# Merge of layer 0 in chunks of 2, 4 and 4 tiles, with merge's first loads beside attention C and the modulation pieces later

## The reference

```
ya = gqa_attend(aq, k_a, v_a)                      # A: 8 heads
yb = diff_attend(bq, k_b, v_b, lam, subln)         # B: 4 heads, RMSNorm over 128 of the output
yc = windowed_latent(cq, ck, cv, xck, xcv, sink)   # C: 8 heads
g  = sigmoid(h @ w_in[gates]); ga, gb, gc = split(g, 3)
m  = ga * (ya @ w_branch_a) + gb * (yb @ w_branch_b) + gc * (yc @ w_branch_c)
x  = x + mod[2] * (m @ w_out)
mod = silu(c) @ w_ada + b_ada                      # one row of 6 * 1024 per layer and token kind
```

## Time and profile before

| what | us |
|---|---|
| median of 3 executions | 5331.33 |
| lowest and highest | 5330.62, 5336.91 |
| the profiled execution, its own time | 5333.29 |
| span of its profile | 5331.7 |
| TensorE busy | 4735.2 (89%) |
| VectorE busy | 3234.0 (61%) |
| ScalarE busy | 2625.5 (49%) |
| POOL busy | 1144.7 (21%) |
| mean granted TensorE clock | 0.948 of full |

### The profile page before, as it was taken

One profiled execution on the slowest core, in us unless ns is written; L12 is line 12 of the kernel. 1 busy time (PEld: TensorE's weight loads), 2 busy tenths in 40 slices (PEclk: granted clock), 3 DMA queues, 4 the chain that ended last, 5 costly groups with the idle time before them and its releaser, 6 DMA issues. The chain is left out here.

```text
span 5331.7 us, 85889 instructions
## 1 busy us (share of the span) xinstructions
PE 4735.2 (89%) x30278; PEld 4027.9 (76%) x30278; DVE 3234.0 (61%) x5512; ACT 2625.5 (49%) x3457; POOL 1144.7 (21%) x1082
## 2 busy tenths in 40 slices
PE   5889899889899977999984888999989998799996
PEld 2788787778678866887774888888868777587774
DVE  4554366767443456877767551667764435777776
ACT  2443355556332322777763442556652321577774
POOL 0542001440000002333333440015100001333333
PEclk7999999999899998999996999999989998899998
DMA  7432533544433455999996433433243327799998
GB/s 276 167 97 79 154 78 81 175 163 108 181 136 126 150 211 190 390 397 397 397 361 236 161 95 99 117 82 77 66 153 132 140 94 241 279 397 397 397 397 336
DMA packets 595821, 1094.75 MB, mean 205 GB/s; under 512 B 112177, under 2 KB 295729, under 8 KB 590497
## 3 DMA queue, kind: packets, MB, share of 16 engines
q1 hardware_dynamic: 551296, 940.52, 51.3%
q0 software_dynamic: 30816, 103.16, 5.1%
q10 hardware_dynamic: 13504, 48.39, 2.3%
HBM read 908.01 MB, written 183.95 MB: 205 GB/s over the span
## 5 line engine op out<-in xcount | busy, mean ns | idle before, releaser
L667 PE MATMUL project_proj_acc<-project_w_split,project_hT 128*128 128x256 f32 x5472 | 730.5, 294 | 3.2 <-DVE project_hT L526 2.9
L667 PEld LDWEIGHTS project_proj_acc<-project_w_split,project_hT 128*128 128x128 f32 x5472 | 699.2, 200 | 7.0 <-DVE project_hT L526 6.6
L1685 PE MATMUL merge_acc<-merge_hT,merge_w_split 128*128 128x512 f32 (+1 forms) x2880 | 641.3, 377 | 37.4 <-DMA merge_hT<-hT 31.0
L1685 PEld LDWEIGHTS merge_acc<-merge_hT,merge_w_split 128*128 128x128 f32 x2880 | 506.5, 191 | 147.6 <-issue 30.5
L2391 DVE TENSOR_TENSOR experts_w_gate<-experts_raw_gate,experts_w_gate 128x2048 fp32r<-128x2048 f32 x148 | 372.2, 2522 | 295.1 <-ACT experts_w_gate L2281 295.1
L2266 POOL TENSOR_TENSOR experts_w_down<-experts_raw_down,experts_w_down 128x2048 fp32r<-128x2048 f32 x74 | 357.2, 4826 | 534.7 <-ACT experts_w_down L2281 534.7
L2440 PE MATMUL experts_gate_acc<-experts_w_gate,experts_rowsT 128*128 128x512 f32 x1776 | 438.1, 402 | 12.8 <-DVE experts_rowsT L2396 7.1
L2454 PE MATMUL experts_result_acc<-experts_w_down,experts_hiddenT 128*128 128x512 f32 x1776 | 436.1, 401 | 12.2 <-DVE experts_w_down L2391 12.2
L971 DVE TENSOR_REDUCE attend_stat<-attend_scores 128x1 f32<-128x1280 f32 (+2 forms) x288 | 305.8, 1062 | 219.2 <-PE attend_scores L872 215.6
L2440 PE MATMUL experts_up_acc<-experts_w_up,experts_rowsT 128*128 128x512 f32 x1776 | 426.5, 395 | 0.0
L2440 PEld LDWEIGHTS experts_gate_acc<-experts_w_gate,experts_rowsT 128*128 128x128 f32 x1776 | 330.9, 190 | 102.7 <-issue 19.8
(11 more groups left out here) (236 smaller groups left out, 8163.8 us busy)
## 6 DMA issues: line engine op xcount, KB each, us to landing
experts_raw_gate<-in_w_exp_gate_dram SPq DMA_DIRECT2D x148, 1024.0 KB, 14.0
experts_raw_up<-in_w_exp_up_dram SPq DMA_DIRECT2D x148, 1024.0 KB, 12.8
experts_raw_down<-in_w_exp_down_dram SPq DMA_DIRECT2D x148, 1024.0 KB, 11.5
merge_w_raw<-in_w_merge_dram SPq DMA_DIRECT2D x120, 768.0 KB, 6.3
qk<-project_staged SPq DMA_DIRECT2D x168, 256.0 KB, 2.3
attend_keys<-qk SPq DMA_DIRECT2D x128, 320.0 KB, 6.0
ye<-experts_result ACTq DMA_DIRECT2D x74, 512.0 KB, 6.3
modulation_w_ada<-in_w_ada_dram SPq DMA_DIRECT2D x24, 1024.0 KB, 26.5
```

What stands on the lines that cost most here:

```text
L667: m = pe.matmul(acc[s % 2][:, 0:HALF], hT[:, a, k, t * P:(t + 1) * P], w_split[hf][:, c, k, :], start=(i == 0 and k == 0), stop=(i == 2 an ...
L1685: m = pe.matmul(acc[:, b, 0:w], w_split[b][:, a, k, :], hT[:, x, k, 0:w], start=(i == 0 and k == 0), stop=(i == 2 and k == KD - 1))
```

## The change

Two buffers now live through attend and merge of a layer. `wide` holds B's keys, then merge's hT; `rows` holds B's probabilities `p0` and `p1`, then merge's three `w_raw`. SP issues hT of tiles 0 to 3 (both halves, 2048 KB each) and the weights of the first three units once B's last step is done, ahead of C's stores and loads; merge itself loads only ident, y and gain before its loop. In both layers the queries and values of A's first head are issued by ScalarE, and SP issues only its keys. In layer 0 POOL waits for step 2 * nq of A's scores before the first two pieces of w_ada. Merge of layer 0 takes its tiles in chunks of 2, 4 and 4; in layer 1 the chunks stay 4 and 4. Since a chunk of two uses only y buffers 0 and 1, the count that a reader of a y buffer waits for is now worked out by `y_load`. The initial y loads stay four.

```diff
+MERGE_ROWS = (KD + 4) * P
@@ attend_gqa, loads
-        def load(i, b):
+        def load_keys(i, b):
...
+        def load_rest(i, b):
             sp.dma_start(queries[b][:, :].bitcast(F32),
...
+        def load(i, b):
+            load_keys(i, b)
+            load_rest(i, b)
@@ sync_first
+            load(0, 0)
+        else:
+            load_keys(0, 0)
         load(0, 1)
+    def scalar_first(act):
+        _, _, load_rest, _ = loads(act)
+        load_rest(0, 0)
@@ attend_b
-    keys = st.sb("b_keys", [P, 2, 2, 2, T], F32R)
+    keys = ahead.wide[:, :].rearrange("p (s c h n) -> p s c h n", s=2, c=2, h=2)
...
-    p0 = [st.sb(f"p0_{b}", [P, T]) for b in range(2)]
-    p1 = [st.sb(f"p1_{b}", [P, T]) for b in range(2)]
+    p0 = [ahead.rows[:, b * T:(b + 1) * T] for b in range(2)]
+    p1 = [ahead.rows[:, (2 + b) * T:(3 + b) * T] for b in range(2)]
@@ attend_b, gpsimd
         if mod:
+            pool.wait_ge(before_it.qk.sem, before_it.qk.done(2 * nq))
             for k in range(mod.RING):
                 mod.load(pool, 0, k)
@@ new functions
+def stage_attend_and_merge(nc, io, scr, l, nq):
+    with ExitStack() as both:
...
+        ahead = Ahead(both.enter_context(nc.sbuf_tensor(f"ahead{l}_wide", [P, 8 * T], F32R)),
+                      both.enter_context(nc.sbuf_tensor(f"ahead{l}_rows", [P, 4 * T], F32)),
+                      [dma(f"hT_{n}_loaded") for n in ("hi", "lo")], [dma(f"w_loaded{b}") for b in range(3)])
+        stage_attend(nc, io, scr, l, nq, ahead)
+        stage_merge(nc, io, scr, l, nq, ahead)
+def load_ahead(io, scr, l, b_last, ahead, sp):
+    sp.wait_ge(b_last.yd.sem, b_last.yd.done(b_last.last))
+    for half in range(2):
+        sp.dma_start(ahead_hT(ahead)[:, half, :, :].bitcast(F32), scr["hT"][half, :, :, 0:512]
+                     ).then_inc(ahead.h_in[half].sem, 16)
+    for b in range(3):
+        sp.dma_start(ahead_weights(ahead, b), io["w_merge"][l, 0, b, :, :, :].rearrange("p k n -> p (k n)")
+                     ).then_inc(ahead.w_in[b].sem, 16)
@@ stage_attend
                 b.sync(sp)
+                load_ahead(io, scr, l, b, ahead, sp)
                 c.sync(sp)
...
             def _(act):
+                a.scalar_first(act)
                 a.scalar(act)
@@ stage_merge
-    chunks = [(0, 4), (4, 4)] + ([(8, 2)] if nq > NL else [])
+    chunks = [(0, 4), (4, 4)] if nq == NL else [(0, 2), (2, 4), (6, 4)]
...
-        hT = st.sb("hT", [P, 2, KD, 512], F32R)
+        hT = ahead_hT(ahead)
...
+        def y_load(c, i):
+            return sum(n > i for _, n in chunks[:c + 1]) - 1
...
                 load_y(0, 0)
-                load_w(0, 0, 0)
-                load_hT(0, 0)
                 load_y(0, 1)
-                load_w(0, 0, 1)
                 sp.dma_start(gain[:, :], io["b_subln"][l].partition_broadcast(P)).then_inc(gain_in.sem, 16)
                 load_y(0, 2)
-                load_hT(0, 1)
                 load_y(0, 3)
-                load_w(0, 0, 2)
...
-                    act.wait_ge(y_in[i].sem, y_in[i].done(c))
+                    act.wait_ge(y_in[i].sem, y_in[i].done(y_load(c, i)))
```

More of the change, by code:

```diff
@@ L703, in __init__ @@
         self.mask0 = (1 if t == 0 else 0) if banded and t < NL else None
-Attention = namedtuple("Attention", "sync_first sync sync_last tensor scalar vector gpsimd qk pv yd last y_out mod")
+Attention = namedtuple("Attention", "sync_first scalar_first sync sync_last tensor scalar vector gpsimd qk pv yd last y_out mod")
 AttentionBuffers = namedtuple("AttentionBuffers", "const_in ident keys queries values probs probsT out stat scores acc "
@@ L801, in store @@
                 :, :, ds(y_col + (i * 2 + b) * HD, HD)], out[b][:, :, :]).then_inc(y_out[b].sem, 16)
-        return load, store
+        return load, load_keys, load_rest, store
     def sync_first(sp):
-        load, _ = loads(sp)
+        load, load_keys, _, _ = loads(sp)
         if banded:
@@ L809, in sync_first @@
             sp.dma_start(sink[:, :], io["c_sink"][l].partition_broadcast(P)).then_inc(band_in.sem, 16)
-        load(0, 0)
+            load(0, 0)
+        else:
+            load_keys(0, 0)
         load(0, 1)
+    def scalar_first(act):
+        _, _, load_rest, _ = loads(act)
+        load_rest(0, 0)
     def sync(sp):
-        load, store = loads(sp)
+        load, _, _, store = loads(sp)
         def body(i):
@@ L1005, in vector @@
         finish(3, NS - 1)
-    return Attention(sync_first, sync, sync_last, tensor, scalar, vector, gpsimd, qk, pv, yd, 4 * NS - 1, y_out, None)
+    return Attention(sync_first, scalar_first, sync, sync_last, tensor, scalar, vector, gpsimd, qk, pv, yd, 4 * NS - 1, y_out, None)
 def lambda_init(l):
@@ L1378, in gpsimd, with dma, ahead_hT, ahead_weights @@
             heads(pool, body)
-    return Attention(sync_first, sync, sync_last, tensor, scalar, vector, gpsimd, qk, pv, yd, NH * nq - 1, y_out, mod)
-def stage_attend(nc, io, scr, l, nq):
+    return Attention(sync_first, None, sync, sync_last, tensor, scalar, vector, gpsimd, qk, pv, yd, NH * nq - 1, y_out, mod)
+Ahead = namedtuple("Ahead", "wide rows h_in w_in")
+def stage_attend_and_merge(nc, io, scr, l, nq):
+    with ExitStack() as both:
+        def dma(name):
+            return Event(Stage.whole_kernel.enter_context(nc.semaphore(f"ahead{l}_{name}")), 0, 16)
+        ahead = Ahead(both.enter_context(nc.sbuf_tensor(f"ahead{l}_wide", [P, 8 * T], F32R)),
[3 more added lines that the diff above has]
+        stage_merge(nc, io, scr, l, nq, ahead)
+def ahead_hT(ahead):
+    return ahead.wide[:, 0:2 * KD * 512].rearrange("p (c k n) -> p c k n", c=2, k=KD)
+def ahead_weights(ahead, b):
+    return ahead.rows[:, b * MERGE_ROWS:(b + 1) * MERGE_ROWS]
+def load_ahead(io, scr, l, b_last, ahead, sp):
[6 more added lines that the diff above has]
+                     ).then_inc(ahead.w_in[b].sem, 16)
+def stage_attend(nc, io, scr, l, nq, ahead):
     with Stage(nc, f"attend{l}") as st:
@@ L1394, in stage_attend @@
         a = attend_gqa(nc, io, scr, l, nq, st, shared, False)
-        b = attend_b(nc, io, scr, l, nq, st, shared, a)
+        b = attend_b(nc, io, scr, l, nq, st, shared, a, ahead)
         c = attend_gqa(nc, io, scr, l, nq, st, shared, True, first=a, before_it=b)
@@ L1432, in _, with stage_merge @@
                 a.gpsimd(pool)
-def stage_merge(nc, io, scr, l, nq):
+def stage_merge(nc, io, scr, l, nq, ahead):
     KB = 4
@@ L1450, in stage_merge @@
         stat = st.sb("stat", [P, 4, 4])
-        w_raw = [st.sb(f"w_raw{b}", [P, KU, P]) for b in range(3)]
+        w_raw = [ahead_weights(ahead, b).rearrange("p (k n) -> p k n", n=P) for b in range(3)]
         w_split = [st.sb(f"w_split{b}", [P, 2, KU, P], F32R) for b in range(3)]
@@ L1459, in stage_merge @@
         const_in, m_out = st.dma("constants_loaded"), st.dma("mT_stored")
-        h_in = [st.dma(f"hT_{n}_loaded") for n in ("hi", "lo")]
+        h_in, w_in = ahead.h_in, ahead.w_in
         gain_in = st.dma("gain_loaded")
         y_in = [st.dma(f"y_loaded{i}") for i in range(4)]
-        w_in = [st.dma(f"w_loaded{b}") for b in range(3)]
         sq, ss, ms, rt, rs, nr, gn = (st.event(n) for n in (
@@ L1701, in turn_y @@
                     else:
-                        pe.wait_ge(y_in[i].sem, y_in[i].done(c))
+                        pe.wait_ge(y_in[i].sem, y_in[i].done(y_load(c, i)))
                     if number >= 2:
```

5 lines of the change are left out of this document (2 added, 3 removed).

## The result

Nine executions of each, side by side: before 5332.47 us (5328.03 to 5336.91), changed 5346.28 us (5339.32 to 5350.0). The ratio is 1.0024, with a 95% interval of 1.0016 to 1.0032: **slower by 0.24%, some 13.8 us**. The forecast was no difference at 5330.4, with a range up to 5341; the time lies above the range, and the sign is that of a case that had 15%.

A forecast was written before the change was run, and what follows sets the result against it. TensorE, busy 89% of the span, was taken to set the pace, so only its waits pay. 7.6 + 0 - 2 + 4.8 + 0.5 - 8 - 2 = 0.9 us; median forecast 5330.4, no measurable difference, range 5318 to 5341.

The forecast's parts named there:

- a case that had 15%: Whole kernel: the outcome that the change makes it measurably slower, given chance 0.15 beside 0.64 same and 0.21 faster.
- Step 1: Start of attention, layer 0: POOL's two modulation loads, issued later, let the first scores come sooner; gain 7.6 us (5 to 9).
- Step 2: Start of attention, both layers: first queries and values on ScalarE's queue; earlier start and added share cancel, 0 (+1.2 to -1.2 us).
- Step 3: Attention C: merge's first loads run beside it, in layer 0 also beside POOL's zero writes; cost 2 us (0 to 6).
- Step 4: Start of merge, layer 1: with hT and weights already there, work up to the norms moves earlier; gain 4.8 us (3 to 6).
- Step 5: Merge, layer 0, chunks of 2, 4, 4: a gain of 0.5 and costs of 8 and 2, 9.5 us lost.
- (a): Merge, layer 0, first output block (f0) of each chunk: sum 114 us instead of 114.5; gain 0.5 (-5 to +4).
- (b): Merge, layer 0, chunk of two: next chunk's y queued ahead of weights delays third output block (f2); cost 8 us (4 to 10).
- (c): End of merge, layer 0, now a chunk of four: longer serial steps, store of twice the size; cost 2 us (1 to 3).
- The slower one: C's second pair, layer 0: zeros and loads ahead at 265 GB/s make keys and queries 24 us late; 5352, chance 0.12.
- The faster one: Merge, layer 0: the short chunk's weights arrive in time and C does not wait; gain 11 us, 5320.4, chance 0.2.
- the three signs: No weight wait in f2 (faster), C waiting over 10 us (slower), or layer 0's first scores 15 us or more after first load.

The follow-up runs named there:

- e5: The kernel before with one edit: POOL waits for step 2 * nq of A's scores before the first two w_ada pieces; 5328.29 us, ratio 0.9987.
- e3: The changed kernel, but in layer 0 merge's first loads are issued behind C's first store and the loads that follow it; 5337.33 us, ratio 1.0005.
- e7: The changed kernel, but in layer 0 y of tiles 4 and 5 is loaded at merge's start, into buffers the chunk of two leaves free; 5339.53 us, ratio 1.0011.
- e11: The changed kernel, but the next chunk's y is issued before the wait for the mT store, and two unread y loads are dropped; 5336.72 us, ratio 1.0002.

## Why the prediction was wrong

**Step 1, pieces later: right.** -7.6 forecast, -7.8 by the medians of e5, within 5 to 9.

**Step 2, first loads on ScalarE's queue: failed.** The step said that "the earlier start and the added share cancel" and took 0, with +1.2 to -1.2 in each layer. The share wins: 2.1 us of wait in layer 1, more than the bound, and with the slow start behind it 3.9 in each layer, 7.8 in all. The step priced the values alone. It left out the second head's keys: with queries and values gone from SP's queue, these keys run beside the first head's. Ahead of the first scores of layer 1 the changed kernel moved 459 long packets and 2.74 MB, the kernel before 387 and 2.34 MB; the 0.40 MB more take 1.8 us at 223 GB/s, nearly the whole 2.1. The values are the smaller part, for 1235 short packets came ahead of the first scores before as well, and 1397 now. No run holds the second head's keys back, so the split rests on these counts. In layer 1 the slow clock behind the longer wait added to it in all eight kernels with the second issuer; in layer 0 the 2.4 GHz level came back within 4.5 us in six of them, so this part is no rule. The Trainium skill's "DMA: Bandwidth & Descriptors", section "Issuing engines are not separate DMA queues", says that the transfers of all issuers run on the same engines and that a second issuer saves only issue time. The trace agrees, no time was gained, and the loss is larger than the 1.2 that the prediction worked out beside it.

**Step 3, first loads beside attention C: failed in layer 0**, right in layer 1, where 6.6 MB cost C nothing. The due time was right: the scores are wanted 46.9 us after the first load ahead, 47 by the step. The landing was not: 55.2 us after it, 45 to 49 forecast. "With both queues served alike" had been read as equal bytes. Here the engines served the queues alike in packets, so zeros of 3.6 KB took 64% of the bytes and loads of 2.0 KB the rest. Cost 10.1 at the wait, where the step had 2 (0 to 6); e3 gave 10 back by the ratio. The 1.3 ahead of C's first store is no part of it, as e3 shows. The Trainium skill's same page, section "Queues, rings and completion order", says that each engine goes round the queues it has work for packet by packet, a packet being some 9 to 17 descriptors. The counts 724 and 725, 878 and 879 agree with turns and not with equal bytes, but 1146 beside 294 at 256-byte rows shows that the packets of the profile are not always taken one for one. The page was in reach before the prediction. The trace of before could not decide it: from 583 to 591 the modulation pieces and the first keys moved 263 and 259 packets, and 1.10 and 1.08 MB, for their packets are nearly of one size.

**Step 4, merge's start in layer 1: right in kind, a little too small**: 6.7 gained where 4.8 (3 to 6) was said; the low-clock price of 0.6 was not seen.

**Step 5, the order 2, 4, 4: right**, 7.4 lost where 9.5 was said. (a) The f0 parts sum to 33.0 + 42.9 + 37.5 = 113.4, 114 forecast. The longer border had been put down to the norms; 1.7 of its 5.4 over the last one are a longer wait for hT. (b) The chunk of two took 102.3 us for f1 to f7 instead of 95.5, 6.8 for the 8 of the step; e7 and e11 show its cause to be the y tiles. (c) The drain went from 5.0 to 6.6, 1.6 for 2.

**The sum.** Putting 10.1 for the 2 of step 3, 7.8 for the 0 of step 2, 6.7 for 4.8 and 7.4 for 9.5 turns +0.9 into 7.6 - 7.8 - 10.1 + 6.7 - 7.4 = -11.0; the medians differ by 13.8. The 1.3 before C's first store and the 2.2 at B's start would make it -14.5, but these two come and go from run to run without an edit, and how often they fall in the nine executions is not known. Steps 2 and 3 are thus the miss, 7.8 and 8.1 us worse than said, against 4.0 better in steps 4 and 5. **The rivals.** The slower one named the right place, C's second pair, but by a rate of 265 GB/s and a wait of 24 us. The rate was 407 GB/s (1160 to 1200) and the wait 8.3, under its deciding 13.6. The kernel is slower all the same, because step 2 was a second loss, which the rivals had priced at 2.4. The faster one falls with the 7.85 us in f2. None of the three signs that the prediction had named for being wrong came: the wait in f2 was there, C waited under 10 us, and the first scores of layer 0 came before 15. It had set them for one large loss, and two middle ones passed below them.

## What to carry to other kernels

Before a load is moved beside other traffic, list which queues are full at that moment and the packet size of each: where packets are taken in turn, as here, the queue with shorter rows gets fewer bytes, and what stands behind it is late by more than bytes over bandwidth. Put the load behind the next one that is due, not ahead of it; and look at what stands ahead of the first need after each issue, since moving four y loads before a store gave back 7 us. Moving one load to another engine's queue also changes what follows in the old one: look at what moves up there. A wait of TensorE at a stage's start can be worth more than its length: in layer 1 the low clock went on longer behind it.

## What was not expected of the hardware

- Two busy queues got 724 and 725, 878 and 879, 766 and 771 packets in 10 us, with 2.64 to 1.45, 3.18 to 0.88 and 2.52 to 1.55 MB. Beside rows of 256 bytes it was 294 and 1146 in 4 us.
- Halving the width of POOL's writes left 2560 packets of 4096 bytes and only added small ones of 4 bytes (2880 to 3200 packets for the same 10.49 MB).
- SP's issue of four loads took 12.34 us behind the 6.6 MB of loads ahead, against 2.70 in the kernel before; the wait shows in the queue's own row first.
- At the start of attention 1 an idle wait of 15.1 to 15.5 us was followed by 12.2 to 12.8 us at 1.2 GHz in all eight kernels with the second issuer, one of 13.2 to 14.1 by 3.5 to 5.2 in the six others. At the start of attention 0 a wait of 16.2 to 16.8 was followed by only 3.7 to 4.5 in six of these eight (in five of them another 3.4 us at 1.2 GHz came soon after), and one of 16.0 and 16.1 by 12.4 and 12.7 in the other two. What sets the moment of the rise was not tested.
